# Handing the last four row tiles of a projection phase to the attention phase behind it

## The reference, cut to what matters

```python
def dilated_mixer(h, w_in, q_norm, k_norm, positions):
    q, k, v, xq = split_cols(h @ w_in, [nh * DIL_HEAD_DIM] * 3 + [D_XA])
    cos, sin = rope_tables(positions, DIL_HEAD_DIM)
    q = apply_rope(rms_norm(hs(q), q_norm), cos, sin)
    k = apply_rope(rms_norm(hs(k), k_norm), cos, sin)
    ...
    for g, (window, dilation) in enumerate(DIL_GROUPS):   # three groups of 4 heads of 128
        o, lse = dilated_window_attention(q[:, :, sl], k[:, :, sl], v[:, :, sl], window, dilation)
    ...
    return o, xq        # xq goes to a cross attention over 256 memory rows, 4 heads of 64
```

## Time and profile before

| what | us |
|---|---|
| median of 3 runs | 2404.55 (2403.34 to 2406.7) |
| the profiled execution's own time | 2405.09 |
| span in its profile, first to last instruction | 2403.3 |
| TensorE busy | 2338.1 (97%) |
| last matmuls of the rows phase to first of da0 | 1516.7 to 1527.9 |
| da0 on TensorE | 1527.9 to 1594.0 |

### The profile page before, as it was taken

The page is one execution under the profiler, slowest core; times in us unless marked ns, Lnnn a source line. Parts: engine busy times, 40 slices in busy tenths (PEclk is TensorE's granted clock), DMA queues, the critical chain, the costliest instruction groups (busy, mean ns, idle before and its releaser), DMA issues. The chain is left out here.

```text
span 2403.3 us, 33350 instructions
## 1 busy us (share of the span) xinstructions
PE 2338.1 (97%) x11988; PEld 2030.3 (84%) x11988; DVE 1888.7 (79%) x2917; ACT 1105.6 (46%) x2217; POOL 221.4 (9%) x252
## 2 busy tenths in 40 slices
PE   8999999999999999999999999798999999999998
PEld 7998877888888888778999999787888888888877
DVE  4422574479999999997998888766779999998996
ACT  6433553344444443446455555665344444444443
POOL 1010012000000002202111111303000000000000
PEclk9999999999999999999999999899999999999999
DMA  4230122222222238963433333745622222227863
GB/s 156 88 98 18 43 86 62 88 72 88 79 79 79 91 112 298 316 199 110 132 113 110 115 106 110 241 139 155 202 82 79 82 94 79 88 79 277 291 184 127
DMA packets 253660, 303.42 MB, mean 126 GB/s; under 512 B 49544, under 2 KB 192888, under 8 KB 253496
## 3 DMA queue, kind: packets, MB, share of 16 engines
q1 hardware_dynamic: 249336, 301.27, 38.2%
q10 hardware_dynamic: 4160, 0.02, 0.1%
HBM read 230.13 MB, written 71.11 MB: 125 GB/s over the span
## 5 line engine op out<-in xcount | busy, mean ns | idle before, releaser
L52 PE MATMUL psum<-f_T_lo 128*128 128x512 f32 x616 | 242.1, 393 | 3.5 <-DVE f_T_lo L698 3.0
L53 PE MATMUL psum<-f_T_lo 128*128 128x512 f32 x616 | 239.9, 389 | 0.0
L54 PE MATMUL psum<-f_T_lo 128*128 128x512 f32 x616 | 239.8, 389 | 0.0
L52 PEld LDWEIGHTS psum<-f_T_lo 128*128 128x128 f32 x616 | 115.6, 188 | 34.5 <-DVE f_T_lo L698 10.8
L52 PE MATMUL psum<-hT_hi,f_up_hi 128*128 128x512 f32 x352 | 137.3, 390 | 0.4 <-DVE f_up_lo L637 0.4
L54 PE MATMUL psum<-hT_hi,f_up_lo 128*128 128x512 f32 x352 | 137.0, 389 | 0.0
L53 PE MATMUL psum<-hT_lo,f_up_hi 128*128 128x512 f32 x352 | 137.0, 389 | 0.0
L54 PEld LDWEIGHTS psum<-f_T_lo 128*128 128x128 f32 x616 | 115.6, 188 | 24.2
L53 PEld LDWEIGHTS psum<-f_T_lo 128*128 128x128 f32 x616 | 115.7, 188 | 23.2
L52 PE MATMUL psum<-p_operand,T_hi 128*128 128x384 f32 x384 | 129.2, 337 | 3.2 <-DVE p_operand L2196 2.5
L54 PE MATMUL psum<-p_operand,token_sums_lo 128*128 128x384 f32 x384 | 128.8, 336 | 0.0
(11 more groups left out here) (501 smaller groups left out, 6674.5 us busy)
## 6 DMA issues: line engine op xcount, KB each, us to landing
raw<-in_ffn_w_up_dram SPq DMA_DIRECT2D x88, 512.0 KB, 4.7
activations<-f_act SPq DMA_DIRECT2D x44, 512.0 KB, 2.6
f_up_pieces<-activations SPq DMA_DIRECT2D x30, 512.0 KB, 5.0
rows_w<-in_b_w_in_dram SPq DMA_DIRECT2D x24, 512.0 KB, 3.8
f_up_pieces<-in_ffn_w_down_dram SPq DMA_DIRECT2D x22, 512.0 KB, 4.8
rows_h<-group_rows SPq DMA_DIRECT2D x14, 768.0 KB, 5.7
group_rows<-raw SPq DMA_DIRECT2D x55, 192.0 KB, 1.8
x_between<-XY SPq DMA_DIRECT2D x16, 512.0 KB, 5.0
```

Of the source, the lines that this page charges most:

```text
L52: nc.tensor.matmul(out, lhs_hi, rhs_hi, start=start, stop=False)
L53: nc.tensor.matmul(out, lhs_hi, rhs_lo, start=False, stop=False)
L54: return nc.tensor.matmul(out, lhs_lo, rhs_hi, start=False, stop=stop)
```

## The change

Tiles 12 to 15 of the last chunk are still combined out of PSUM in the rows phase, but no longer squared, rotated, scaled or stored there. A new class `LeftOver` does it in da0: ScalarE squares tile `n` at `i` = 1, 3, 5, 7 and scales it at `i` = 6, 9, 12, 15; VectorE rotates it at `i` = 4, 7, 10, 13; GpSimd makes the roots of two tiles at a time, in program order behind the cross queries' four instructions; SP stores them among its other transfers. The cos and sin tables of the keys are loaded again (two DMAs) into two tiles of `XY`, ahead of the stores of tiles 6 to 8. The wait at da0's start covers only the first two groups' stores; the wait for all stands behind the last handed tile. Rooms that must outlive the phase are allocated one level out.

```diff
-LAST_ROTATED_IN = {3: (0, 1), 4: (2, 3), 5: (4, 5), 6: (6, 7, 8, 9, 10, 11), 7: (12, 13, 14, 15)}
+LAST_SQUARED_IN = {2: (0, 1, 2, 3), 5: (4, 5, 6, 7), 6: (8, 9, 10, 11)}
+LAST_ROTATED_IN = {3: (0, 1), 4: (2, 3), 5: (4, 5), 6: (6, 7, 8, 9, 10, 11)}
-LAST_SCALED_IN = {4: (0, 1), 5: (2, 3), 6: (4, 5), 7: (9, 10, 11), 8: (12, 13, 14, 15)}
+LAST_SCALED_IN = {4: (0, 1), 5: (2, 3), 6: (4, 5), 7: (9, 10, 11)}
+LEFT_OVER = (12, 13, 14, 15)
...
                 if m == LASTM - 1:
+                    sp.wait_ge(p_done, product(CH - 1, W22))
+                    left.load(sp)
                     for q in SCALED_LATE:
                         store(CH - 1, q)
                 if m == LASTM:
-                    sp.wait_ge(p_done, product(CH - 1, W22))
...
-                for quads in ROOTS:
+                for quads in ROOTS if c + 1 < CH else ROOTS[:5]:
...
+class LeftOver:
+    def act(self, act, i):
+        n = (i - 1) // 2
+        if i % 2 and n < len(LEFT_OVER):
+            s, j = self.group(n)
+            if n:
+                act.wait_ge(self.squared, n)
+            for h in range(2):
+                cols = slice(h * P, (h + 1) * P)
+                ins = self.nc.scalar.activation(self.squares_room[:, cols], self.slot(n)[:, cols], ACT.Square, accum_out=self.sums[:, s, 2 * j + h:2 * j + h + 1])
+            ins.then_inc(self.squared, 1)
+        n = (i - 6) // 3
+        if i % 3 == 0 and 0 <= n < len(LEFT_OVER):
+            s, j = self.group(n)
+            act.wait_ge(self.roped, n + 1)
+            act.wait_ge(self.rooted, s + 1)
+            for h in range(2):
+                cols = slice(h * P, (h + 1) * P)
+                ins = self.nc.scalar.activation(self.slot(n)[:, cols], self.slot(n)[:, cols], ACT.Copy, scale=self.rstd[:, s, 2 * j + h:2 * j + h + 1])
+            ins.then_inc(self.scaled, 1)
+    def dve(self, dve, i):
+        n = (i - 4) // 3
...
+    def pool(self, pool):
+        for g in range(2):
+            sums, rstd = self.sums[:, g, 0:4], self.rstd[:, g, 0:4]
+            pool.wait_ge(self.squared, 2 * g + 2)
+            self.nc.gpsimd.tensor_scalar(sums, sums, 1.0 / P, EPS, ALU.mult, ALU.add).then_inc(self.mean, 1)
+            pool.wait_ge(self.mean, g + 1)
+            self.nc.gpsimd.tensor_tensor(rstd, sums, self.neg_half[:, 0:4], ALU.pow).then_inc(self.rooted, 1)
...
 attention_phase, VectorE loop
                     tiles.cross[2].dve(dve)
+                if left:
+                    left.dve(dve, i)
 attention_phase, ScalarE loop
                 tiles.act_next(act, i)
+                if left:
+                    left.act(act, i)
 attention_phase, SP
                 row_loads(sp, t)
+                if left:
+                    for n in range((t - 1) // 2, t // 2) if t >= 2 else ():
+                        left_store(sp, n)
 attention_phase, GpSimd
                 tiles.cross[2].pool(pool)
+                left.pool(pool)
```

More of the change, by code:

```diff
@@ L1869, in rows_phase @@
                squares_room, small,
-               first_rows, rows_loaded, xq_load, ident, qT, kT):
+               first_rows, rows_loaded, xq_load, ident, qT, kT, first_operand, slot_room, left):
     DH = DC // 2
@@ L1897, in operand_room @@
             return x[:, 0, :, :], x[:, 1, :, :], raw[:, 1, :, :]
-        first_operand = operand_room(0)
-        slot_room = sb("slots", [P, 3, BLOCK])
         squares = [sb("squares", [P, ROPED]), squares_room]
@@ L1970, in squared_in @@
         def squared_in(m):
-            return due(SQUARED_IN, SQUARED_IN, m)
+            return due(SQUARED_IN, LAST_SQUARED_IN, m)
         def rotated_in(m):
@@ L2352, in _, with __init__, load, number @@
                 turn_heads(nc, turn_bank(n), first_rows(t)[0], of_keys, ident).then_inc(tile_turned, 1)
+class LeftOver:
+    def __init__(self, nc, ctx, raws, slot_room, small, squares, neg_half, cos, sin, tables):
+        self.nc, self.neg_half, self.squares_room, self.tables = nc, neg_half, squares, tables
+        self.slot_room, self.raws, self.cos, self.sin = slot_room, raws, cos, sin
+        self.sums, self.rstd = (small[:, x:x + 24].rearrange("p (s h) -> p s h", h=6) for x in (0, 24))
+        self.loaded, self.squared, self.mean, self.rooted, self.crossed, self.turned, self.roped, self.scaled = (
+            phase_semaphore(nc, ctx, f"left_{n}") for n in ("loaded", "squared", "mean", "rooted", "crossed", "turned", "roped", "scaled"))
+    def load(self, sp):
+        for table, d in zip((self.cos, self.sin), self.tables):
+            sp.dma_start(table, d).then_inc(self.loaded, 16)
+    def number(self, n):
+        return TT + 16 * 5 + LEFT_OVER[n]
+    def slot(self, n):
+        s = self.number(n) % RING
+        return self.slot_room[:, s, :] if s < 3 else self.raws.tiles[(s - 3) // 2][:, (s - 3) % 2 * BLOCK:((s - 3) % 2 + 1) * BLOCK]
+    def cross(self, n):
+        return self.raws.tiles[n % 2][:, 2 * BLOCK:]
+    def token_tile(self, n):
+        q = LEFT_OVER[n]
+        return (0, 4, 0, 4)[q // 4] + q % 4
+    def group(self, n):
+        return n // 2, n % 2
+    def act(self, act, i):
[19 more added lines that the diff above has]
+        n = (i - 4) // 3
+        if i % 3 != 1 or not 0 <= n < len(LEFT_OVER):
+            return
+        if n == 0:
+            dve.wait_ge(self.loaded, 32)
+        if n >= 2:
+            dve.wait_ge(self.roped, n - 1)
+        t = self.token_tile(n)
+        tile = slice(t * P, (t + 1) * P)
+        x, rows = (self.slot(n)[:, 0:ROPED].rearrange("p (h two k) -> p h two k", two=2, k=P // 2), self.slot(n)[:, 0:ROPED])
+        y = self.cross(n).rearrange("p (h two k) -> p h two k", two=2, k=P // 2)
+        s = self.sin[:, tile].rearrange("p (two k) -> p two k", two=2)
+        for two in range(2):
+            ins = self.nc.vector.tensor_tensor(y[:, :, two, :], x[:, :, 1 - two, :], s[:, 1 - two, :].unsqueeze(1).broadcast_to([P, 2, P // 2]), ALU.mult)
+        ins.then_inc(self.crossed, 1)
+        dve.wait_ge(self.crossed, n + 1)
+        dve.wait_ge(self.squared, n + 1)
+        heads = rows.rearrange("p (h n) -> p h n", n=P)
+        self.nc.vector.tensor_tensor(heads, heads, self.cos[:, tile].unsqueeze(1).broadcast_to([P, 2, P]), ALU.mult).then_inc(self.turned, 1)
+        dve.wait_ge(self.turned, n + 1)
+        self.nc.vector.tensor_tensor(rows, rows, self.cross(n), ALU.add).then_inc(self.roped, 1)
+    def pool(self, pool):
[5 more added lines that the diff above has]
+            self.nc.gpsimd.tensor_tensor(rstd, sums, self.neg_half[:, 0:4], ALU.pow).then_inc(self.rooted, 1)
+    def store(self, sp, n, rows, stored):
+        k, t = self.number(n), self.token_tile(n)
+        b = 2 + (0, 1, 1, 0)[LEFT_OVER[n] // 4]
+        sp.wait_ge(self.scaled, n + 1)
+        sp.dma_start(rows[t * P:(t + 1) * P, b * BLOCK:(b + 1) * BLOCK], self.slot(n)).then_inc(stored[k % RING], 16)
@@ L2489, in dve_next, with attention_phase @@
             self.dve_keys(dve, self.job(i)[0])
-def attention_phase(nc, ph, psum, ident, units, stage, turns_of, row_loads, loads=(), ahead=None, room=(), merge=None):
+def attention_phase(nc, ph, psum, ident, units, stage, turns_of, row_loads, loads=(), ahead=None, room=(), merge=None, left=None, left_store=None):
     U = len(units)
@@ L2699, in _ @@
                 stage.store_sums(sp)
+            if left:
+                for n in range(TT // 2 - 1, len(LEFT_OVER)):
+                    left_store(sp, n)
         if ahead is not None:
@@ L4064, in build @@
             rooms = [rows_w[:, i, :].rearrange("p (d n) -> p d n", d=DC // 2) for i in range(4)]
+            with ExitStack() as same_place:
+                raw = sb("first_operand_sum", [P, 2, DC // 2, BLOCK], F32, same_place)
+            with ExitStack() as same_place:
+                x = sb("first_operand", [P, 2, DC // 2, BLOCK], F32R, same_place)
+            first_operand = x[:, 0, :, :], x[:, 1, :, :], raw[:, 1, :, :]
+            rows_g = sb("rows_g", [P, 2, 4 * BLOCK], F32, rows_ctx)
+            slot_room = sb("row_slots", [P, 3, BLOCK], F32, rows_ctx)
+            left = LeftOver(nc, c, raws, slot_room, small_room, squares_room, neg_half, XY[:, TT - 2, :], XY[:, TT - 1, :], tables_d[1])
             rows_phase(nc, "p1", psum, neg_half, hT_hi, hT_lo, h_room, T_hi, sum_lo, sum_room, rooms, raws, begun, w, order, tables_d, rows_d, xq_d, row_stored, squares_room, small_room, lambda t: row_load(0, t), rows_loaded[0],
-                       load_xq, ident, qT, kT)
-            rows_g = sb("rows_g", [P, 2, 4 * BLOCK], F32, rows_ctx)
+                       load_xq, ident, qT, kT, first_operand, slot_room, left)
             stage = Stage(nc, c1, order, outs_d, sums_d)
@@ L4072, in load_rows, with wait_rows, left_store @@
                 sp.dma_start(out, src).then_inc(rows_loaded[n % 2][t], 16)
+            def wait_rows(sp, groups):
+                for s in range(RING):
+                    sp.wait_ge(row_stored[s], 16 * len(range(s, TT + 16 * 2 * groups, RING)))
+            def left_store(sp, n):
```

(11 more changed lines are left out.)

## The result

| | before | after |
|---|---|---|
| median of 6 runs each, us | 2405.20 (2403.34 to 2406.70) | 2415.47 (2413.52 to 2418.96) |
| ratio | | 1.0047, 95% interval 1.0034 to 1.0059 |
| span of the profiled execution, us | 2403.3 | 2413.7 |
| its granted clock | 0.993 | 0.991 |
| last matmul of the rows phase to first of the second attention, us | 1516.68 to 1594.88: 78.20 | 1517.57 to 1606.73: 89.16 |

The kernel is slower by 10.3 us. The last line of the table is the stretch that the change touches; it grew by 10.96 us. It will serve as the yardstick for the experiments, because it leaves out what an execution does elsewhere. This one reached the seam 0.89 us later than that of before; the two were 0.84 us apart already at a pause in the first layer (383.99 and 384.83), and behind the stretch this one won some 1.5 us back. I did not follow that up. Each stretch comes from one execution.

The account below looks back on a forecast made before the run. At the seam the block, not data, held TensorE; inside da0 TensorE is nearly full, so delays stay. Terms 6.5 + 1.1 + 1.2 = +8.8 us on 2404.55 gave 2413.35; 8-in-10 range 2408.5 to 2416.5.

Parts of the forecast that it names:

- Term 3: TensorE's clock falls to half around the gate in da0, about 2.5 us outside the stall: +1.2 us (0 to 2.6).
- Term 1: At i = 6 ScalarE's first handed scale waits for GpSimd's root, delaying unit 7's exponential: +6.5 us.
- The phase's end: Seam before da0: SP's last load becomes the last end, so da0 starts at 1522.27, 5.65 us earlier.
- The zero for the earlier start: At i = 2 ScalarE still waits for the cross queries' load, so da0's earlier start gains zero.
- free mixing: Alternative for the cross queries' load: queued bytes mix, so the removed stores' going gains it 2.1 us.
- the cited rule: Trainium skill: each DMA engine consumes descriptors in ring order, so removing later stores gains the cross queries' load nothing.
- Term 2: VectorE's handed rotations in da0, mainly at i = 13 where it is nearly full: +1.1 us (0 to 2.4).
- The gate was not open: Rival at i = 6: GpSimd's chain ends by 1543, ScalarE finds the root made; 2406, no change; chance 0.08.
- the load did not land earlier: Rival: cross queries land 5.65 us sooner and GpSimd's chain with them; +3.1 us, 2407.7; chance 0.04.
- TensorE's lead: Rival: TensorE needs only unit 7's exponential, so its lead swallows part of the wait; +4.5, 2409.0; chance 0.07.
- The port case: Rival: GpSimd stands still during VectorE's rotations at i = 4 and 7, chain 2.7 us later; 2416.0; chance 0.08.

Follow-up runs that it names:

- e5: Changed kernel, with TensorE doing 44 identity turns while it waits for ScalarE's exponential of unit 7; 2412.12 us, ratio 1.0030 to the kernel before.
- e7: Changed kernel without the four handed tiles' squares, roots, rotations and scales; tables, loads and waits stay; 2406.30 us, ratio 1.0003 to the kernel before.
- e1: Changed kernel, with the first handed root moved behind the first of GpSimd's four cross-query instructions; 2411.69 us, ratio 1.0021 to the kernel before.
- e3: Changed kernel, first root behind GpSimd's first cross-query instruction, cross queries' load ahead of stores and row loads; 2401.50 us, ratio 0.9976 to the kernel before.
- e8: Changed kernel with nothing computed for the four handed tiles and the cross queries' load issued first; 2396.78 us, ratio 0.9968 to the kernel before.
- e9: As e3, with the second handed tile's rotation moved from i = 7 to i = 8; 2403.17 us, ratio 1.0002 to the kernel before.

## Where the prediction held, and the step that failed

The direction and both mechanisms hold: the load ate the earlier start, and the root behind the long chain shut a gate. What failed is the size of two terms of the sum. The step that failed most is Term 3, the clock: "part of it inside the stall, I take about 2.5 us outside", so +1.2 us. The trace shows 8.4 us outside the stall, and e5 prices them at 2.4 us, twice the term. Term 1, the gate, was put at +6.5 us and measures 7.5.

The measured 2415.47 is 2.1 us above the forecast of 2413.35. Of these, 0.65 are the median of before, which six runs put at 2405.20 and three at 2404.55; the change itself cost 10.3 us in time where the sum said 8.8. On the stretch it cost 10.96, so the sum was 2.2 us short there, with both errors the same way, and the time came nearer to it by the 0.7 us that this execution won elsewhere, which is luck. Step by step:

- **The phase's end.** Predicted 5.65 us earlier, measured 11.24 - 5.55 = 5.69. Right. The two table loads went out at 1510.10 and 1510.58, but took 3.8 and 4.6 us to land, up to 1515.2, and were not gone before the stores issued at 1513.88. It cost nothing that shows: those stores took 1.8 us to landing, as before, and the cross load 11.7, as before.
- **The zero for the earlier start.** Right: the square at 1532.96 without the shift, and e7. The removed stores had not held the load up, since it takes 11.7 us to landing in both kernels; the 2.1 us of a free mixing did not come, as the cited rule had it. The wait was 5.79 where I said 6.35, since ScalarE also squared a handed tile before it.
- **Term 1, the gate, 6.5 us: right in place, short by 1.0.** The root was to be there at 1550.5 and the exponential of unit 7 at 1551.2; without the shift the latter came at 1551.94. GpSimd's chain took 14.32 us for 14.05, the root 1.60 for 1.38, and ScalarE started 0.39 us behind it. The lag at the turn of the next keys was 1556.11 - 0.89 - 1547.74 = 7.5 us. I had also given TensorE 0.3 us back that it did not win. ScalarE stood 6.41 us where I said 3 to 5, as its own work reached the gate less late than I had assumed.
- **Term 3, the clock, 1.2 us: half of what it is.** Between that turn and the first cross turn (1563.63 against 1552.80, less the shift: 9.94) the lag grows by 2.5 us, and e5 takes 2.41 us away by keeping the clock up. I had 3.4 to 5.8 us for the whole stay at half clock, from two places of the trace of before: 3.4 is the whole stay after a pause of 2.25 us, but 5.8 is only its part behind a restart. Here the clock was down for 10.2 us. TensorE worked from 1553.74, stood again for 0.82 us, and came back to 1.00 some 6.0 us behind its second restart at 1556.11, close to the 5.8 of before; that the further pause drew it out is not shown.
- **Term 2, the rotations, 1.1 us.** At i = 13 the lag grows from 9.94 us to 10.96 at the first cross unit (1570.85 against 1559.00, less the shift): 1.0 us, with the pause of 0.89 us on the cross turn. Those at i = 4 and 7 end before the gate opens, and the one at i = 10 adds nothing that shows between the two lags above. Where there is no gate they are dearer: the handed work costs 2.4 us of stretch with the load late (e1 against e7) and 3.2 with it early (e3 against e8).
- **The rivals.** The gate was not open (e1 shows what it would have been), and the load did not land earlier. TensorE's lead did not help, the shared bank held it. The port case had its direction wrong: GpSimd's chain grew by 0.27 us only, and it is VectorE that stood still (below). Its 2416.0 is nearer to the measured time than the forecast, by chance.

Put together from the runs, in steps from one kernel to the next, which add up by construction: 0.4 us for the seam with nothing handed (e7), 2.4 for the handed work (e1 against e7), 5.7 for the gate at full clock (e5 against e1), 2.4 for the clock behind it (e5): 10.96. The gate is thus three quarters of the loss, and it is a matter of where one pair of small GpSimd instructions stands.

## What to carry to other kernels

When work is moved over a phase's end, look for what each engine in the next phase waits for first: here an earlier start was worth nothing until the transfer that ends the first wait was issued earlier too. A small instruction put behind long ones on a seldom used engine becomes a gate if an engine on the path needs its result in order; its place in the queue costs more than its duration. Price each stall twice, once for its length and once for TensorE's clock behind it.

## What the hardware showed that I had not expected

A VectorE instruction that reads two SBUF tiles did not run beside GpSimd's long two-input instruction; it ended only when GpSimd's had. VectorE in the changed kernel, the rotations at i = 7 and i = 10:
```profile
1547.18 3.33 DVE L2421 TENSOR_TENSOR raw<-raw,XY 128x128 f32<-128x128 f32 x2
...
1558.88 0.48 DVE L2421 TENSOR_TENSOR raw<-raw,XY 128x128 f32<-128x128 f32 x2
```
The first ran while GpSimd's L2477 did, which ended at 1550.16, and lasted 3.33 us in place of 0.48; e9 repeats it with 3.87 in place of 0.42. In both, GpSimd's instruction had begun first (1546.54, and 1540.58 against 1540.61), and it took its usual 3.62 us. Copies from PSUM and the masked maximum, with one tile in SBUF, ran beside the same GpSimd instruction at their usual length. Beside GpSimd's power of 32 columns a rotation took its usual time, as GpSimd and VectorE in e3 show:
```profile
1534.98 5.42 POOL L2477 TENSOR_TENSOR small_room<-small_room,neg_half 128x32 f32<-128x32 f32 x1
```
```profile
1539.24 0.48 DVE L2422 TENSOR_TENSOR raw<-raw,XY 128x128 f32<-128x128 f32 x2
```
The Trainium skill ("GPSIMD Engine Reference", section "Specifications") names contention for this pair, when VectorE reads two SBUF inputs. The traces agree for GpSimd's instruction over 2048 columns, where VectorE waited for all that was left of it; for the power over 32 columns they show no wait.

The second is how unlike two stays at half clock can be: with the pause of 5.22 us came 10.2 us at 0.50, and with the one of 5.55 us, in the same kernel, 6.8 us, each counted from the clock's fall inside the pause.
